# Seven block products for each pair of feed-forward input blocks, with the low parts of the weights subtracted on VectorE

## The reference, cut to what matters

```python
def swiglu(h, w_in, w_out):
    gu = h @ w_in
    gate, up = gu[..., :D_FF], gu[..., D_FF:]
    return (jax.nn.silu(gate) * up) @ w_out
...
for i in range(DEPTH):                        # DEPTH = 2, D_MODEL = 1024, D_FF = 2816
    h_res = h_res + 0.5 * swiglu(rms_norm(h_res, ffn1_norm[i]), ffn1_w_in[i], ffn1_w_out[i])
    h = rms_norm(h_res, mix_norm[i])
    ...                                       # convolution branch, attention branch, gates, w_out
    h_res = h_res + 0.5 * swiglu(rms_norm(h_res, ffn2_norm[i]), ffn2_w_in[i], ffn2_w_out[i])
return h_res[:, N_META:]                      # 16 + 512 = 528 tokens, 512 come back
```

## Time and profile before

| | us |
|---|---|
| median of 3 runs (2509.07 to 2511.03) | 2510.64 |
| the profiled execution | 2510.25 |
| its span, first to last instruction | 2508.1 |
| PE busy in it | 2486.4 (99%) |
| weight loads on PE, beside the matmuls | 2317.2 (92%) |
| DVE busy | 994.1 (40%) |
| ACT busy | 935.7 (37%) |
| POOL busy | 588.1 (23%) |

### The profile page before, as it was taken

One profiled execution on the slowest core, in us unless ns is written; L12 is line 12 of the kernel. 1 busy time (PEld: TensorE's weight loads), 2 busy tenths in 40 slices (PEclk: granted clock), 3 DMA queues, 4 the chain that ended last, 5 costly groups with the idle time before them and its releaser, 6 DMA issues.

```text
span 2508.1 us, 41815 instructions
## 1 busy us (share of the span) xinstructions
PE 2486.4 (99%) x17865; PEld 2317.2 (92%) x17865; DVE 994.1 (40%) x1530; ACT 935.7 (37%) x1422; POOL 588.1 (23%) x825
## 2 busy tenths in 40 slices
PE   7999999999999999999999999999999999999999
PEld 7999999999999999999999999999888778888887
DVE  3222112788885332221122221127988853322200
ACT  5333223343345344432233342224433453443311
POOL 2222222111212222222222222221212122222222
PEclk9999999999999999999999999999999999999999
DMA  8888888666667888888888888886766689889997
GB/s 198 181 180 175 180 179 179 131 144 137 136 136 162 178 179 179 176 179 176 184 179 180 178 178 177 182 181 138 153 136 142 131 178 189 186 188 187 190 198 167
DMA packets 120935, 426.89 MB, mean 170 GB/s; under 512 B 13680, under 2 KB 13680, under 8 KB 120816
## 3 DMA queue, kind: packets, MB, share of 16 engines
q0 software_dynamic: 117504, 419.48, 79.1%
q1 hardware_dynamic: 2944, 5.34, 0.7%
q10 hardware_dynamic: 368, 0.33, 0.0%
HBM read 421.92 MB, written 2.10 MB: 169 GB/s over the span
## 4 chain that ended last, share of the span: by engine, by line
PE 97%; DMA 1%; ACT 1%; DVE 0%; issue 0%; POOL 0%; ACTq 0%; DVEq 0%
PE po L677 91%; PE pov L804 1%; PE pov L802 1%; PE ptr L783 1%; PE pstat L767 1%; DMA wl<-in_weights 1%; PE pov L739 1%; PE pstat L769 0%; PE pstat L742 0%; PE ptr L785 0%; DMA sink<-in_sinks 0%; ACT cv L640 0%; PE ptr L745 0%; PE pstat L692 0%; DMA wh<-in_weights 0%; ACT xh L643 0%
## 5 line engine op out<-in xcount | busy, mean ns | idle before, releaser
L677 PE MATMUL po<-xh,wh 128*128 128x264 f32 (+1 forms) x3872 | 918.9, 306 | 14.6 <-DVE xl L909 14.0
L677 PE MATMUL po<-xl,wh 128*128 128x264 f32 (+1 forms) x3872 | 911.4, 304 | 0.0
L677 PE MATMUL po<-xh,wl 128*128 128x264 f32 (+1 forms) x3872 | 908.6, 303 | 0.0
L418 ACT ACTIVATE wl<-wh 128x1024 fp32r<-128x1024 f32 (+1 forms) x408 | 425.0, 1042 | 1119.5 <-DMA wh<-in_weights 1119.4
L677 PEld LDWEIGHTS po<-xh,wh 128*128 128x128 f32 x3872 | 626.7, 190 | 45.8 <-issue 14.7
L677 PEld LDWEIGHTS po<-xl,wh 128*128 128x128 f32 x3872 | 625.5, 190 | 25.8 <-issue 0.2
L677 PEld LDWEIGHTS po<-xh,wl 128*128 128x128 f32 x3872 | 624.9, 190 | 26.4
L394 POOL DMA_DIRECT2D wh<-in_weights x408 | 223.7, 548 | 1752.8 <-PE po L677 1713.1
L399 POOL DMA_DIRECT2D wl<-in_weights x408 | 366.6, 899 | 151.3 <-ACT wl L418 135.4
L1004 DVE SCALAR_TENSOR_TENSOR cv<-ub,lp,cv 128x528 f32<-128x528 f32 (+1 forms) x480 | 333.2, 752 | 1.7
L677 PE MATMUL po<-hh,wh 128*128 128x264 f32 (+1 forms) x1232 | 283.2, 299 | 0.2
(11 more groups left out here) (152 smaller groups left out, 1749.1 us busy)
## 6 DMA issues: line engine op xcount, KB each, us to landing
wh<-in_weights POOLq DMA_DIRECT2D x376, 512.0 KB, 5.0
wl<-in_weights POOLq DMA_DIRECT2D x376, 512.0 KB, 7.4
wh<-in_weights POOLq DMA_DIRECT2D x32, 384.0 KB, 3.9
wl<-in_weights POOLq DMA_DIRECT2D x32, 384.0 KB, 6.7
resid<-in_x SPq DMA_DIRECT2D x8, 264.0 KB, 7.4
out<-resid SPq DMA_DIRECT2D x8, 256.0 KB, 5.9
kn<-kn SPq DMA_DIRECT2D x8, 132.0 KB, 2.2
prm<-in_params ACTq DMA_DIRECT2D x1, 312.0 KB, 4.3
```

Source lines behind the costliest of these rows:

```text
L418: func(wl[:, s, 0:k, :], wh[:, s, 0:k, :].bitcast(F32), ACT.Copy, scale=-1.0).then_inc(w_neg, 1)
L677: ins = mm(po[:, 2 * out_slot + h, 0:width], w[:, s, k, :], v[:, k, t:t + width], start=begin and k == 0 and w is wh and v is mh_, stop=la ...
```

## The change

The 22 pairs of a feed-forward are cut in three chunks of 7, 7 and 8 pairs, and after each chunk come 8 output blocks over that chunk's 7 or 8 tile depths, added to the residual at once. A pair's gate and up blocks, split in even and odd input tiles, times the activations, split the same way and in two halves of the tokens, is a two by two by two product of blocks. It is no longer made of eight block products but of seven, P1 to P7, on sums of blocks. One block product is 4 tile depths by three matmuls by 264 columns (256 in the last feed-forward), 12 matmuls, so a pair has 84 matmuls where it had 96 (of 264 columns), or 84 of 256 where it had 48 of 512.

The sums of the weights are made in the kernel. `pairs` brings 1 MB for a pair through SP (`load_pair`, into `raw`, two buffers); VectorE makes four sums of 128x512 (`sum12`, `sum43`); ACT copies each to its high part (`sum_hi`, `base_hi`, `base22_hi`); VectorE subtracts for the low part (`sum_lo`, `base_lo`, `base22_lo`), and also for the output blocks (`out_lo`). The second, adding transfer is left to the mixers. The seven activation operands are made at the start of a stage, tile pair by tile pair, by `x7_parts` on ACT and `x7_operands` on VectorE through one buffer `tmp`. The results of P1, P5 and P6 are copied from PSUM by ACT (`copy_e1`, `copy_e5`, `copy_e6`) and joined on VectorE (`gate`, `up2`, `inner`) before the Silu and after it. The mixers are the same but for the place of their first three `neg`. All loops are unrolled.

The core of the diff (`+` after, `-` before; the rest of it renames buffers and counts):

```diff
-OUT_K = ((0, KD), (KD, 2 * KD), (2 * KD, KF))
-SLOTS = 4
+CHUNKS = ((0, 7), (7, 14), (14, KF))
+PRODUCT = {"P1": (U_A, 0, B11), "P2": (U_A, 1, B21), "P3": (U_S43, 0, B22), "P4": (U_A22, 0, T4),
+           "P5": (U_S12, 0, T1), "P6": (U_S12, 1, T2), "P7": (U_S43, 1, T3)}
...
+            def copy_e1(j):
+
+                act.wait_ge(blk_used, USED["P1", j])
+                act.wait_ge(c12_taken, j)
+                func(scratch(j)[4], x_bank(j), ACT.Copy).then_inc(e1_done, 1)
...
+            def x7_parts(l, which, s, m, gain):
...
+                if m > 1:
+                    act.wait_ge(x7_lo, (s * KP + kp) * 2)
...
+                    for j in range(j0, j1):
+                        if j > j0:
+                            silu(j - 1)
+                        if j + 1 < j1:
+                            sum_hi(j + 1, 0)
+                        copy_e1(j)
+                        if j + 2 < j1:
+                            base_hi(j + 2)
...
+                        copy_e5(j)
+                        if j == s * KF:
+                            std(l, 2 * f)
...
+            def sum12(j):
...
+                tt(s12[:, 0:KP, :], tile4(0), tile4(3), ALU.add).then_inc(s_sum, 1)
+                dve.wait_ge(s_sum, 4 * j + 1)
+                tt(s12[:, KP:, :], tile4(1), s12[:, 0:KP, :], ALU.add).then_inc(s_sum, 1)
...
+            def gate(j, h):
...
+                if h == 0:
+                    dve.wait_ge(blk_used, USED["P2", j])
+                    dve.wait_ge(e1_done, j + 1)
+                    dve.wait_ge(silu_done, j)
+                    tt(g, y_bank(j), copy, ALU.add).then_inc(c11_taken, 1)
+                    if j % KF == 0:
+                        rms_of(j // (2 * KF), 2 * (j // KF % 2))
...
+                    for j in range(j0, j1):
+                        if j + 1 < j1:
+                            sum12(j + 1)
+                        gate(j, 0)
+                        if j == s * KF and f == 0:
+                            layer_params(l)
+                        if j > j0:
+                            up2(j - 1)
+                        if j + 1 < j1:
+                            sum43(j + 1)
+                            sum_lo(j + 1, 0)
+                            sum_lo(j + 1, 1)
+                        else:
+                            out_lo(s, c, 0)
+                        if j + 2 < j1 or j + 1 == j1 and more:
+                            base_lo(j + 2 if j + 2 < j1 else j1)
+                        if j > j0:
+                            inner(j - 1)
+                        if j + 1 == j1:
+                            out_lo(s, c, 1)
+                        gate(j, 1)
+                        if j + 1 < j1:
+                            base22_lo(j + 1)
+                        if j > j0:
+                            inner_lo(j - 1)
```

More of the change, by code:

```diff
@@ new lines, in begins, with run_of, regions, tensor_order @@
+def begins(s):
+    return s % 2 == 1 or s == 0
+def run_of(j):
+    s = j // KF
+    while not begins(s):
+        s -= 1
+    e = s + 1
+    while e < STAGES and not begins(e):
+        e += 1
+    return s * KF, e * KF
+def regions():
+    out, r = [], 1
+    for s in range(STAGES):
+        if begins(s):
+            r = 1
+        for a, b in CHUNKS:
+            out += [r ^ i & 1 for i in range(b - a)]
+            r = out[-1]
+    return out
+REGION = regions()
+def tensor_order():
+    for s in range(STAGES):
+        for c, (a, b) in enumerate(CHUNKS):
+            for j in range(s * KF + a, s * KF + b):
+                yield "P1", j
+                yield "P2", j
+                if j > s * KF + a:
+                    yield "P7", j - 1
+                yield "P5", j
+                yield "P6", j
+                if j > s * KF + a:
+                    yield "P4", j - 1
+                yield "P3", j
+            yield "P7", s * KF + b - 1
+            yield "P4", s * KF + b - 1
+            for m in range(KD):
+                yield "out", s, c, m
+        if s % 2 == 0:
+            for n in range(NBLK):
+                yield "mix", s // 2, n
@@ L164, in build @@
-def build(nc, x, params, qk_gain, sinks, weights, weights6, out):
+    return "w_in", (({A: 0, B: O_B, GA: O_GA, GB: O_GB}[kind] + j * P, P),)
+def build(nc, x, params, qk_gain, sinks, pairs, outs7, outs8, mixes, out):
     rows = lambda w: w.rearrange("l (k p) n -> p l k n", p=P)
@@ L569, in _ @@
                         std(l, 1)
+                        neg(l, B_MIX + 2)
                     h(0)
@@ L716, in ffn_out @@
[L716 to L724 removed]
+                return lambda k: pe.wait_ge(x_lo, l * KD + k + 1)
@@ L918, in layer_params @@
+            base_lo(0)
+            for k in range(KD):
+                x7_operands(0, 0, 0, k)
+                if k == 1:
+                    base22_lo(0)
+                if k == 5:
+                    base_lo(1)
+                if k == 4:
+                    sum12(0)
+                    sum43(0)
+                if k == 6:
+                    sum_lo(0, 0)
+            sum_lo(0, 1)
             def layer_params(l):
                 dve.wait_ge(x_sq, norm(l, 0) * KD + KD)
-                dve.wait_ge(x_lo, norm(l, 0) * KD + KD)
+                dve.wait_ge(x7_lo, (2 * l + 1) * KD)
@@ new lines, in mixer_out @@
+            def mixer_out(l):
+                j0 = (2 * l + 1) * KF
+                post = l == LAST
+                nc.vector.memset(acc_m, 0.0).then_inc(acc_done, 2)
+                for m in range(KD):
+                    if m == 1:
+                        sum12(j0)
+                        sum43(j0)
+                        base_lo(j0)
+                    if m == 6:
+                        base22_lo(j0)
+                    if m == 7:
+                        base_lo(j0 + 1)
+                    if m in (2, 3):
+                        sum_lo(j0, m - 2)
+                    ready(l, B_MO + m)
+                    stt(cols(resid[:, m, :], post), slot(ps(m), post), 0.5, cols(resid[:, m, :], post), ALU.mult,
+                        ALU.add).then_inc(out_taken, 1)
+                    x7_operands(l, 2, 2 * l + 1, m)
```

798 lines of the change are left out of this document (577 added, 221 removed).

## The result

The changed kernel takes 2532.07 us (median of 4 runs, 2528.59 to 2536.34), the kernel before 2509.86 in the same comparison (4 runs, 2505.44 to 2511.03): a ratio of 1.0093, 95% interval 1.0073 to 1.0112. It does an eighth less matrix work in the feed-forwards' input blocks and is 0.9% slower; the forecast was 2530.0. The profiled execution took 2528.59 us, with a span of 2526.5 against 2508.1.

A forecast was written before the change was run, and what follows sets the result against it. PE, busy 99%, bounds the kernel before; after the change VectorE sets the pace. Costs of 62.5 us less 42.7 saved give 19.8 slower: 2510.25 + 19.8 = 2530.0 us, range 2485 to 2590.

The forecast's parts named there:

- The pair inside a chunk: Full pair on VectorE: 11.42 us summed against 11.75 before, with a 1.5 us stall for the copy of P1's result.
- PE's own pace: PE alone in a pair: seven products need 10.20 us, and PE waits 1.2 us a pair at P6 for VectorE's pace.
- Chunks: Chunks of 7 and 8 pairs: 118.6 and 135.8 us, last stage 116.1 and 132.9; together 42.7 us saved.
- Starts after a mixer: Feed-forward start after a mixer: 9.2 us lost, twice, 18.4; PE idle 6 us ahead of P7, the reciprocal at 11.5.
- From ffn2 to ffn1: Between ffn2 and ffn1: operands made inside the output blocks and the layer parameters cost 9.2 + 3.8 + 0.9 = 14 us.
- The program's start: First feed-forward's start: some 23 us lost; single buffer `tmp` makes turns cost 5.9 us for each of four tile pairs.
- Mixers: Mixers: late third `neg` costs 2.2 us, twice, 4.4, with adding transfer of 7.4; raw weights beside the convolution's weights 2.
- Rival 1: In pairs: P1's copy is not late and PE sets the pace at 10.3 us, 72 us off, 2458; chance 0.12.
- Rival 2: At stage starts: ScalarE and VectorE overlap better, half of the 55 us of the starts goes, 2503; chance 0.13.
- Rival 3: On VectorE: each instruction spaced by its full duration, 1.1 us more a pair, 70 us, 2600; chance 0.08.
- the rule of the Trainium skill: On VectorE: next instruction starts only when the pipe is empty; a pair's thirteen free starts would each come 0.08 later.
- Rival 4: PE goes to half pace after gaps: 3 us each stage start, or 3100 if gaps of 1.2 us do it; chance 0.02.

The follow-up runs named there:

- early copy: Changed kernel with ScalarE copying P1's result before it makes the high part of the next pair's first sum: 2460.61 us, ratio 0.9809 to the kernel before.
- less work on VectorE: Changed kernel with `base_lo` subtracting 512 of 1024 columns, except in the first four pairs of a run: 2499.87 us, ratio 0.9970 to the kernel before.
- less work on TensorE: Changed kernel without the low-weight matmuls of P2 and P3, 76 matmuls a pair instead of 84: 2522.64 us, ratio 1.0054 to the kernel before.
- early negative: Changed kernel with each mixer's third `neg` before ScalarE's Sqrt instead of behind it: 2529.83 us, ratio 1.0081 to the kernel before.
- both edits: Changed kernel with P1's copy ahead of the sum's high part, and Sqrt and reciprocal later at stage starts: 2436.69 us, ratio 0.9711 to the kernel before.

## Why the prediction came out, point by point

- **The pair inside a chunk.** Held: 11.42 summed, 11.44 measured; the stall 1.5 and 1.46; the copy behind `sum_hi` behind `sum12`. That it is what makes the pair long, and not only where the wait shows, is shown by the early copy (10.27), by less work on VectorE (10.90) and by less work on TensorE (11.43). In the last stage it is 11.36 (2286.49 to 2297.85 on the same line) for 11.34.
- **PE's own pace.** 10.20 was summed and 10.27 is what it keeps when it never waits. PE's wait at P6 is 0.94, not 1.2: 0.07 of the rest is PE's pace, and the first matmul after a gap is followed by the next only 0.23 us later (80.69 to 80.92) instead of 0.12. The remaining tenth I can't place.
- **Chunks.** Low by a little each: 119.13 for 118.6, 136.7 for 135.8, in the last stage 116.63 and 133.45 for 116.1 and 132.9. Over twelve chunks these are 7.4 us; the term "42.7 us saved" measured some 35.
- **Starts after a mixer.** Held: from MO's last residual step to the end of the first chunk 129.3 (by the steps 128.7) and 126.6 (126.2); the gap of PE 6.20 for 6, the reciprocal 11.4 us after that residual step, for 11.5 after PE's end. The wait for the Sqrt is 2.75 us, where 2 was named as the sign; it is the part that a reordering takes away.
- **From ffn2 to ffn1.** 14 summed; the last chunk is 2.7 and the next one 11.9 us longer than their like, 14.7.
- **The program's start.** The time held (gate at 40.87 for 41.5, end of the first chunk at 162.93 for 55.2 - 11.3 + 118.6 = 162.5), the reason did not: VectorE's own work, not the single buffer, fills it.
- **Mixers.** The step that failed: 6.4 us summed for the late third `neg` and the raw transfers, -2.8 measured. The adding transfer took 6.5 us by its median instead of 7.4 and PE hardly waited. In layer 0 this is all there is to it: the mixer is 0.2 us longer, for 3.2. That the mixer of layer 1 is 3.0 us shorter goes with the clock and not with the change, as far as the windows show. In the kernel before, the granted clock fell in the mixer of layer 1, and in the changed kernel's profiled execution it did not at the same place (first a window of before, then one of after):

```profile
1843.82:1902.47 58.65, 58.65 (x391) 50.87 (x390) 50.99 (x85) 24.74 (x59) 11.62 (x16) 0.94 0.69 147
```

```profile
1854.49:1912.78 58.29, 58.29 (x409) 51.28 (x408) 52.29 (x88) 27.23 (x66) 11.55 (x16) 1.00 0.72 152
```

  PE is busy throughout both; (1.00 - 0.94) x 58.65 = 3.5 us, about the 3.0 by which the stretch is shorter. In the profiled execution with the early negative (2536.26 us) the clock was 0.96 to 0.98 over nearly all of both mixers, as in this window of its second one, where the changed kernel had 1.00:

```profile
1750.00:1850.00 100.00, 100.00 (x672) 85.19 (x671) 80.42 (x133) 41.79 (x105) 18.96 (x26) 0.97 0.63 133
```

  So a term of two or three microseconds in a mixer can't be judged by the stretch's length, only by PE's waits.
- **Rivals 1 and 2.** Rival 1 did not occur, but it is one exchange away, as shown. Rival 2, cheaper starts, did not either: the starts cost what was summed, to within a microsecond each.
- **Rival 3, full-duration spacing, and the rule of the Trainium skill.** Refuted: in the rows of the pair above, 1352 starts 0.34 us after 1453, which lasts 0.42, and the same holds for each free start. By the Trainium skill, "VectorE: DVE Perf Modes", section "The DRAIN you can't avoid", the next instruction waits for an empty pipe; in this trace it regularly starts 0.08 us before the last one ends, and the rule's own exception (an instruction that is not held) is the usual case here.
- **Rival 4, half pace.** Gaps of 0.94 us in each pair did nothing to the clock (1.00 in the window above). Behind the 6.20 us gap it stood at 1.2 GHz. As the prediction had it, this lies where PE waits for VectorE in any case, so I take it to cost little in the changed kernel; no run here removes it alone. With the early copy, where PE sets the pace behind the start, it does count.

## What to carry to other kernels

When an engine that goes in order gets two duties, put the short one that somebody waits for ahead of the long one that itself waits: here 0.37 us of copy behind a wait for another engine cost 71 us (2532.07 - 2460.61), of the 129 that the saved matmuls are worth by the prediction's sum. Sum the list of each engine for one period before trading matmuls for elementwise work; with 10.27 against 9.89 us the trade pays, and of a further cut of 85 us on TensorE alone only some 45 reach the time. Gains at a start and in the steady state are not independent: what a start costs depends on whether the late engine can catch up afterwards, and on whether the engine that sets the pace comes back from its idle time at full clock.

## What the runs showed of the hardware

After an idle stretch of 6.20 us TensorE came back at half clock (1.2 GHz). Busy us and granted clock of the changed kernel in four stretches behind it:

```profile
925.00:926.00 1.00, 0.95 (x4) 0.98 (x5) 1.00 (x3) 0.59 (x1) 0.00 (x0) 0.50 0.00 0
926.00:927.00 1.00, 1.00 (x7) 1.00 (x6) 0.97 (x2) 0.05 (x1) 0.00 (x0) 0.50 0.04 6
...
928.00:930.00 2.00, 2.00 (x17) 2.00 (x16) 1.21 (x4) 1.62 (x3) 0.00 (x0) 0.87 0.08 30
930.00:935.00 5.00, 5.00 (x44) 5.00 (x43) 5.00 (x8) 2.36 (x4) 0.00 (x0) 1.00 0.49 161
```

The length of the gap alone does not tell whether the clock falls: in the kernel with both edits it stayed at 1.00 at the program's start, behind gaps of up to 1.75 us, and was 0.50 from 902 to 904 us, behind one of 1.74 us at the second start. What I had not expected is that the clock also falls while PE is busy without a gap: 0.80 in a stretch of ten us of the kernel before,

```profile
1853.00:1863.00 10.00, 10.00 (x52) 7.80 (x51) 5.99 (x11) 4.38 (x9) 1.45 (x2) 0.80 0.90 196
```

and not at the same place in every execution. The four runs of the changed kernel, with a mean granted clock of 0.988, 0.986, 0.985 and 0.984, had spans of 2526.5, 2529.9, 2529.9 and 2534.2 us: much of the scatter between runs of one kernel goes with the clock. What makes it fall there stays open. At a program's start the granted clock is no guide: it stands at 1.00 from 17 to 21 us in the kernel before, where the matmuls go at half pace by the earlier trace rows.
